# Squares of q's first block and the norm of the latent keys in small pieces on ScalarE, the keys' transposes inside the index loop

## The reference

```
n = rms_norm(h, norm1_g)
q_att, c_kv, q_idx, k_idx, w_idx, r_q, r_k, r_v, r_gate, g_att, g_ret = split(n @ w_in)
q = rms_norm(q_att.reshape(B, S, 8, 128), q_norm_g)
kv = rms_norm(c_kv, kv_norm_g) @ w_kv_up
k_sh, v_sh = split(kv, 2)
k_sh = rms_norm(k_sh, k_norm_g)
k_idx = rms_norm(k_idx, idx_k_norm_g)
dots  = einsum('bqhd,bsd->bqhs', q_idx, k_idx) * IDX_DIM ** -0.5
score = einsum('bqhs,bqh->bqs', relu(dots), w_idx)      # causal, then top_k(score, 256)
logits = einsum('bqhd,bqkd->bhqk', q, k_sel) - slopes * dist
```

## Time and profile before

| | |
|---|---|
| median of 3 runs | 1596.65 us (1596.41 to 1597.43) |
| profiled execution, its own time | 1592.75 us |
| its span, first to last instruction | 1590.9 us |
| TensorE busy | 1464.6 us, 92% |
| VectorE busy | 1093.0 us, 69% |
| ScalarE busy | 768.1 us, 48% |
| POOL busy | 494.7 us, 31% |
| mean granted TensorE clock | 0.964 |

### The profile page before, as it was taken

One profiled execution on the slowest core, in us unless ns is written; L12 is line 12 of the kernel. 1 busy time (PEld: TensorE's weight loads), 2 busy tenths in 40 slices (PEclk: granted clock), 3 DMA queues, 4 the chain that ended last, 5 costly groups with the idle time before them and its releaser, 6 DMA issues.

```text
span 1590.9 us, 19861 instructions
## 1 busy us (share of the span) xinstructions
PE 1464.6 (92%) x7190; PEld 1210.8 (76%) x7190; DVE 1093.0 (69%) x1530; ACT 768.1 (48%) x1247; POOL 494.7 (31%) x365
## 2 busy tenths in 40 slices
PE   5989899998999797999999999999996699999895
PEld 5978788986889686677687888888874677877784
DVE  4328999999999467765378843336354778988783
ACT  5237223337322626766442442333244577878783
POOL 2310121470524135100145543332241234544421
PEclk9999999999999997999999999999998799999998
DMA  5200121112221112210246334434434788798775
GB/s 191 61 27 1 34 49 39 40 41 93 80 53 41 41 40 94 80 41 14 67 150 200 95 132 147 151 139 143 165 116 177 274 296 262 189 297 252 241 229 128
DMA packets 87216, 195.19 MB, mean 123 GB/s; under 512 B 11088, under 2 KB 32848, under 8 KB 84816
## 3 DMA queue, kind: packets, MB, share of 16 engines
q1 hardware_dynamic: 74448, 153.56, 28.8%
q0 software_dynamic: 8928, 32.51, 8.5%
q10 hardware_dynamic: 3744, 7.87, 1.3%
HBM read 200.71 MB, written 37.22 MB: 150 GB/s over the span
## 4 chain that ended last, share of the span: by engine, by line
PE 70%; DVE 10%; DMA 8%; ACT 5%; issue 3%; SPq 1%; POOL 1%; ACTq 0%; DVEq 0%; POOLq 0%
PE ps L718 20%; PE ps L720 19%; PE ps L719 19%; PE ps L940 4%; DMA e_raw<-in_w_up 3%; DVE dist L1576 2%; DMA out<-e_y,dest 2%; PE ps L930 2%; DVE e_lo L1961 2%; PE ps L1049 1%; DMA w_raw<-in_w_in 1%; ACT junk L1227 1%; DMA xin<-in_x 1%; DVE f_sum L1694 1%; PE ps L883 1%
## 5 line engine op out<-in xcount | busy, mean ns | idle before, releaser
L2018 POOL TENSOR_TENSOR w_lo<-w_raw,w_hi 128x512 fp32r<-128x512 f32 (+1 forms) x184 | 257.1, 1403 | 642.4 <-ACT w_hi L1117 641.8
L1117 ACT CAST w_hi<-w_raw 128x512 fp32r<-128x512 f32 (+1 forms) x184 | 111.9, 615 | 419.2 <-PE ps L720 369.2
L718 PE MATMUL ps<-w_hi,n_hi 128*128 128x512 f32 (+2 forms) x704 | 246.2, 350 | 8.6 <-POOL w_lo L2018 6.8
L719 PE MATMUL ps<-w_lo,n_hi 128*128 128x512 f32 (+2 forms) x704 | 243.4, 346 | 0.0
L720 PE MATMUL ps<-w_hi,n_lo 128*128 128x512 f32 (+2 forms) x704 | 243.2, 346 | 0.0
L1961 DVE TENSOR_TENSOR e_lo<-e_raw,e_hi 128x2048 fp32r<-128x2048 f32 x93 | 210.1, 2286 | 28.7 <-ACT e_hi L1468 27.2
L1468 ACT CAST e_hi<-e_raw 128x2048 fp32r<-128x2048 f32 x93 | 176.3, 1916 | 67.0 <-DMA e_raw<-in_w_up 66.8
L1613 DVE MAX8 small<-dist 128x8 f32<-128x384 f32 (+5 forms) x192 | 171.8, 895 | 6.6
L1614 DVE MATCH_REPLACE8 dist<-small,dist 128x384 f32<-128x384 f32 (+5 forms) x192 | 168.1, 876 | 0.0
L718 PE MATMUL ps<-n_hi,w_hi 128*128 128x512 f32 x416 | 164.2, 395 | 3.0 <-POOL w_lo L2018 2.9
L719 PE MATMUL ps<-n_lo,w_hi 128*128 128x512 f32 x416 | 162.3, 390 | 0.0
(11 more groups left out here) (272 smaller groups left out, 2872.1 us busy)
## 6 DMA issues: line engine op xcount, KB each, us to landing
e_raw<-in_w_gate SPq DMA_DIRECT2D x62, 512.0 KB
e_raw<-in_w_up SPq DMA_DIRECT2D x62, 512.0 KB
e_raw<-in_w_down SPq DMA_DIRECT2D x31, 1024.0 KB
w_raw<-in_w_in SPq DMA_DIRECT2D x120, 256.0 KB, 2.7
a_raw<-att_dram SPq DMA_DIRECT2D x16, 512.0 KB, 3.4
a_raw<-ret_dram SPq DMA_DIRECT2D x16, 512.0 KB, 3.4
w_raw<-in_w_out SPq DMA_DIRECT2D x24, 256.0 KB, 3.2
w_raw<-in_w_in SPq DMA_DIRECT2D x40, 128.0 KB, 2.3
```

The source lines that it names most:

```text
L718: mm(out, a[0], b[0], start=first, stop=False, skip_group_check=skip)
L719: mm(out, a[0], b[1], start=False, stop=False, skip_group_check=skip)
L1117: nc.scalar.copy(w_hi[c % NH][:, :width], split_from(c)[:, :width]).then_inc(hi_ready, 1)
L2018: G.tensor_tensor(w_lo[c % NH][:, :width], split_from(c)[:, :width], w_hi[c % NH][:, :width].bitcast(F32), ALU.subtract).then_inc(lo_ready, 1)
```

## The change

Three things are rearranged.

1. The norm of the latent keys. Squares and scaling leave VectorE. ScalarE squares and sums tile h's keys after the relu of step (3, h) (`square_k`), and scales them after the relu of step (4, h) (`norm_k`); `norm_k(0)` waits for POOL, whose two instructions now follow the last square. `k_sq` and `k_n` count to 8.
2. The keys' transposes. TensorE's eight, ScalarE's `kT_hi` and VectorE's `kT_lo` move from behind the index loop to the start of t = 6 (`KT_TILE`). So that they find banks 6 and 7, the strips of t = 2 to 5 begin with bank pair 6, 7 instead of 0, 1.
3. q's squares. `square_q0(t)` now does one tile, after ScalarE's cast at chunk t of gate1.

```diff
+        k_junk = [r1t(f"k_junk{i}", [P, DH], 2624 + i * DH) for i in range(2)]
...
+        KT_TILE = 6
         for t in range(2, NT):
+            if t == KT_TILE:
+                for half in range(2):
+                    bk.use(("kT", half), 6 + half)
             for h in range(HI):
-                bk.use(("idx", t, h), 2 * (h % 4), 2)
-        for half in range(2):
-            bk.use(("kT", half), 6 + half)
+                bk.use(("idx", t, h), 2 * ((h + (3 if t < KT_TILE else 0)) % 4), 2)
...
+            def turn_k():
+                pe.wait_ge(k_n, NT)
+                for half in range(2):
+                    bk.wait_free(pe, ("kT", half))
+                    for t in range(4):
+                        last = tr(bank(("kT", half))[:, t * P:(t + 1) * P], kvu[:, 4 * half + t, 0:DH], ident)
+                    bk.filled(last, ("kT", half))
...
             for t in range(2, NT):
+                if t == KT_TILE:
+                    turn_k()
...
-            pe.wait_ge(k_n, 1)
-            for half in range(2):
-                bk.wait_free(pe, ("kT", half))
-                for t in range(4):
-                    last = tr(bank(("kT", half))[:, t * P:(t + 1) * P], kvu[:, 4 * half + t, 0:DH], ident)
-                bk.filled(last, ("kT", half))
...
+            def square_k(t):
+                if t == 0:
+                    for i in range(4):
+                        bk.wait_read(act, ("kvu", i))
+                if t >= 2:
+                    act.wait_ge(k_sq, t - 1)
+                A(k_junk[t % 2][:], kvu[:, t, 0:DH], ACT.Square, accum_out=small[:, 48 + t:49 + t]).then_inc(k_sq, 1)
+
+            def norm_k(t):
+                if t == 0:
+                    act.wait_ge(k_rstd, 1)
+                A(kvu[:, t, 0:DH], kvu[:, t, 0:DH], ACT.Identity, scale=small[:, 56 + t:57 + t]).then_inc(k_n, 1)
...
             for t in range(2, NT):
+                if t == KT_TILE:
+                    turn_k()
...
                     bk.read(A(relu[n % 2][:, :nk], ps[:, c:c + nk], ACT.Relu), name)
                     n += 1
+                    if t == 3:
+                        square_k(h)
+                    if t == 4:
+                        norm_k(h)
...
             def out_block(name):
-                ahead(name)
+                for k in range(KT):
+                    hi(number[name] * KT + k + NH - 1)
+                    if name == "gate1":
+                        square_q0(k)
...
-                if (what, m) == ("phase2", 1):
-                    square_q0()
...
-            ksq = sq[:].rearrange("p t d -> p (t d)")[:, 0:S].rearrange("p (t d) -> p t d", d=DH)
-            seq(V.tensor_tensor(ksq, kvu[:, :, 0:DH], kvu[:, :, 0:DH], ALU.mult))
-            V.tensor_reduce(small[:, 48:56], ksq, X, ALU.add).then_inc(k_sq, 1)
-            dve.wait_ge(k_rstd, 1)
-            V.tensor_tensor(kvu[:, :, 0:DH], kvu[:, :, 0:DH], small[:, 56:64].unsqueeze(2).to_broadcast([P, NT, DH]), ALU.mult).then_inc(k_n, 1)
...
             for t in range(2, NT):
+                if t == KT_TILE:
+                    lo_kT()
...
-            pool.wait_ge(k_sq, 1)
+            pool.wait_ge(k_sq, NT)
```

More of the change, by code:

```diff
@@ L1167, in _, with turn_k @@
                 bk.read(nc.scalar.copy(kvu[:, 2 * i:2 * i + 2, :].rearrange("p t d -> p (t d)"), bank(name)), name)
+            def square_k(t):
[9 more added lines that the diff above has]
+                A(kvu[:, t, 0:DH], kvu[:, t, 0:DH], ACT.Identity, scale=small[:, 56 + t:57 + t]).then_inc(k_n, 1)
+            def turn_k():
+                for half in range(2):
+                    name = ("kT", half)
+                    bk.wait_full(act, name)
+                    A(kT_hi[:, half * BANK:(half + 1) * BANK], bank(name), ACT.Identity,
+                      scale=gains[:, GK:GK + 1]).then_inc(kT_hi_done, 1)
             n = 0
             for t in range(2, NT):
+                if t == KT_TILE:
+                    turn_k()
                 nk = (t + 1) * P
@@ L1178, in _ @@
                     n += 1
-            for half in range(2):
-                name = ("kT", half)
-                bk.wait_full(act, name)
-                A(kT_hi[:, half * BANK:(half + 1) * BANK], bank(name), ACT.Identity,
-                  scale=gains[:, GK:GK + 1]).then_inc(kT_hi_done, 1)
+                    if t == 3:
+                        square_k(h)
+                    if t == 4:
+                        norm_k(h)
             def out_gate(p):
@@ L1614, in take_rounds @@
                     seq(V.match_replace(sc, m8, sc, TAKEN))
-            for half in range(2):
-                name = ("kT", half)
-                dve.wait_ge(kT_hi_done, half + 1)
-                bk.read(V.scalar_tensor_tensor(kT_lo[:, 4 * half:4 * half + 4], bank(name).rearrange("p (t k) -> p t k", k=P), gains[:, GK:GK + 1],
-                                               kT_hi[:, half * BANK:(half + 1) * BANK].rearrange("p (t k) -> p t k", k=P).bitcast(F32),
-                                               ALU.mult, ALU.subtract), name)
             for t in range(NT):
```

30 lines of the change are left out of this document (17 added, 13 removed).

## The result

The change took 1579.05 us (median of 4 runs, 1577.75 to 1580.16) against 1596.53 us of the kernel before in the same comparison (4 runs, 1595.24 to 1597.43): ratio 0.9898, 95% interval 0.9885 to 0.9911, a gain of 17.5 us. The forecast was 1579.9 with a range of 1576.0 to 1587.0 and faster at 0.95: right, and most of its terms can be found again in the trace. Two of them can't: the squares of k were mis-sized, and VectorE's slack before head 2 came out half as wide as forecast. One sentence of it failed as well: the granted clock in the index loop did not rise. That the time came within 0.9 us of the forecast is partly luck.

What follows compares the result with a forecast made beforehand. TensorE, busy for 92% of the span, was taken as the bound between 110 and 620 us. Gate0 -7.1, gate1 -10.1 and its end +0.4 summed to -16.8 us: 1579.9 us from the median of 1596.65, range 1576 to 1587.

Steps and rivals of the forecast that it cites:

- squares of k, t = 3: Index loop, t = 3: eight squares on ScalarE lengthen the steps, +1.4 us, bounds 0.7 and 2.
- POOL's wait: Index loop before t = 4: ScalarE's first scaling waits for POOL and delays VectorE, +1.9 us, from 1.0 to 3.0.
- gate0's first chunk (A): Behind the index loop: gate0's first chunk ends at 167.6 instead of 174.7, -7.1 us, bounds -5 and -8.5.
- gate1: Block gate1: the cast ahead of q's squares removes 6.97 us of waiting and 3.1 of low clock, -10.1 us.
- end of gate1: Behind gate1's last cast: the last four squares delay the Silu, TensorE may be late, +0.4 us.
- VectorE's wait left at 543: Before head 2: VectorE's 19.4 us wait for POOL shrinks by 15.0, leaving 4.4 us.
- The clock in the loop: Index loop's start: without TensorE's 4.56 us wait the half clock of 119 to 125 us goes, hidden behind VectorE's pace.
- The turn's place: Keys' turn at t = 6: transposes hidden, the 4.0 us wait gone, gate0 follows at once at full clock.
- Rival (c): Index loop: the clock falls and the kernel gets slower, +33 us if t = 3 to 7 ran at 1.2 GHz; chance 0.03.
- (a): Rival, index loop: it gives back what it gains, so gate0 gains nothing, time 1587; chance 0.10.
- (b): Rival, before head 2: VectorE becomes the bound at 543, time 1581 to 1585; chance 0.04.
- (d): Rival, gate1: the stall is only moved, POOL or ScalarE late one chunk later, 1586 to 1590; chance 0.03.

Runs made afterwards that it cites:

- e6: Changed kernel with each square of k in the index loop taken a second time into an unread buffer; 1578.0 us, one run.
- e4: Changed kernel with the keys' turn back behind the index loop and the old bank order; ratio 0.9926 to the kernel before.
- e0: The changed kernel itself, run again without edits; ratio 0.9892 to the kernel before, median 1578.08 us.
- e2: Changed kernel with q's squares back in one block ahead of gate1; ratio 0.9956 to the kernel before.
- e3: Changed kernel with squares, sums and scaling of k back on VectorE ahead of the loop; ratio 0.9918 to the kernel before.
- e5: Changed kernel with the eight scalings of k three steps later; ratio 0.9878 to the kernel before, median 1575.33 us.
- e7: Changed kernel with four more max instructions on VectorE before round 0 of the last tile's top-k; 1581.47 us, one run.
- e10: The kernel of e5 (changed kernel, scalings of k three steps later) run again beside e9; ratio 0.9882 to the kernel before, median 1578.03 us.
- e9: The changed kernel itself a third time, without edits, as partner of e10; ratio 0.9885 to the kernel before, median 1578.45 us.
- e1: Kernel before with part 3 alone, q's squares four at a time behind gate1's casts; ratio 0.9944 to the kernel before.

## Why the prediction was right, point by point

| term (changes in us, measured in the changed kernel's first profile) | predicted | measured |
|---|---|---|
| VectorE's start | -5.1 | -5.25 |
| t = 2 | 0 | +0.42 |
| squares of k, t = 3 | +1.4 | 0 |
| POOL's wait, t = 4 | +1.9 | +1.86 |
| `kT_lo` in the loop | +1.5 | +1.33 |
| last relu, the sum of those above | -0.3 | -1.66 |
| gate0's first chunk (A), loop included | -7.1 | -8.25 |
| gate1 | -10.1 | -9.95 |
| end of gate1 | +0.4 | 0 |
| A, gate1 and its end together | -16.8 | -18.2 |
| VectorE's wait left at 543 | 4.4 | 2.32 |

- **The step that was mis-sized** is "Relu and square together are 1.03 us, 0.17 us over the step". It added the relu's full duration to the squares' spacing in gate1. In that row each square waits for the one before; in the loop neighbours overlap by 0.1 us at both ends. The prediction had the overlap in hand (it used it for the scalings, from four casts in 2.18 us) and didn't apply it to the squares. The eight squares at t = 3 cost 0 us instead of 1.4. That is more than the 1.15 us by which A was better than forecast; the pause at t = 2 took 0.42 back. e6 shows the right price.
- **POOL's wait** was right in sum, for slightly other reasons. POOL's first instruction took 0.70 us instead of the 0.20 of the earlier trace rows, so ScalarE stood still 1.91 us and not 1.35. With the first scaling, 0.31 from its start to the relu's, ScalarE was 2.22 us late, and VectorE passed on 1.86 of them. The prediction's own parts, 1.35 and 0.30, add up to less than its 1.9. Its sentence that ScalarE can't catch up within t = 4 was wrong: behind the stall the relus start 0.88 us apart, against a step of 0.98.
- **The clock in the loop** is the sentence that failed. The prediction had the end of TensorE's wait of 4.56 us remove the half clock of 119 to 125 us. The wait went, and the half clock came all the same, at 121 to 127 us and twice more. It had put its price at nothing, as VectorE sets the pace, and that held up to t = 5.
- **The turn's place**, with gate0 following at once, was right: a TensorE wait of 3.99 us, the transposes at low clock and the low clock behind them went together, and the row of e4 brings them back. The transposes inside the loop hid as forecast, with `kT_lo` ending TensorE's one longer wait there, 1.44 us, after it had made three strips of t = 6. The Trainium skill's rule that transposes don't count as work for the clock gate (TensorE: Matmul & The Clock Gate, Part 4: PE-mode transpose) would have allowed a fall there that costs time. There is a low stretch at 147 to 151 us, behind the transposes, in the changed kernel, and one near it in e0, e2, e3, e5 and e7 to e10; e4, without transposes in the loop, has none there, which agrees with the rule. But e4 lacks the wait for `kT_lo` as well, and the low stretch begins in that wait or right behind it, 4 to 7 us behind the transposes, with strips between them; e6, with both, has none. So it isn't settled which of the two brings it. The price was nil in the changed kernel's first execution and 0.4 us in e0 and 0.3 in e9, under the 1.6 us that the prediction had named for this rule.
- **Rival (c)** was right in its mechanism and wrong in its price. The clock fell inside the loop as the Trainium skill warns (TensorE: Matmul & The Clock Gate, A second HAM failure mode: psum-queue depth-cycling), but TensorE runs up to four bank pairs ahead and VectorE sets the pace, so 0.67 over 10 us and 0.89 over the next 33 cost the changed kernel nothing one can find, and e0 and e9 0.3 to 0.4 us. The prediction's sum for a clock of 1.2 GHz throughout shows why: by it a step of t = 3 takes TensorE 1.28 us (an eighth of 10.2) against VectorE's 0.86, so each step at half clock uses up 0.42 us of TensorE's lead, and only then is VectorE late. Whether short pauses bring the clock down, as that section says of another kernel, no run here shows.
- **The end of gate1** cost nothing, as the eight Silu ran in 4.03 us behind full banks instead of 5.31.
- **Spread in the sum.** The 18.2 us are 1.4 more than forecast, but about 1.5 of them hang on the longer half clock in before's one profile of gate1 (see e2), and in e0 and e9 the shift at B is 17.2 us.
- **The slack at 543** came out 2.1 us smaller than forecast: TensorE gained 1.4 us more than its sum, and VectorE's rounds ended only 1.1 us earlier, not 1.8. VectorE's rows about the loop's end show where its time went, changed kernel:

```profile
166.31 1.27 DVE L1608 TENSOR_TENSOR dist<-dist,cst 128x128 f32<-128x128 f32 x1
167.61 1.20 DVE L1649 TENSOR_SCALAR dist<-cst 128x128 f32<-128x128 f32 x1
168.85 0.29 DVE L1650 TENSOR_TENSOR dist<-dist,cst 128x128 f32<-128x128 f32 x1
```

POOL beside them:

```profile
165.20 3.53 POOL L2040 TENSOR_TENSOR w_lo<-w_raw,w_hi 128x512 fp32r<-128x512 f32 x2 [37.62 <-ACT w_hi L1124]
```

The mask addition takes 0.29 us in every other key tile and 1.27 here, where POOL is splitting weights; POOL's two, one row here, take 2.23 and 1.34 us instead of 1.29. Before, the mask addition ran with POOL idle; the row of 1.20 us behind it is no loss, as before it took 1.25, also beside a split of POOL's. The same happens once more at 385.49, where VectorE's 768 wide `SCALAR_TENSOR_TENSOR` (L1664) takes 1.93 us against 0.96 before, under POOL's instruction at 385.12. The rounds' own `MAX8` and `MATCH_REPLACE8` show nothing of the kind. Work of POOL's that now lies beside these two instructions thus took about 2 us from VectorE; that the two engines exclude each other there is read from these rows and not tried by an experiment.

The other rivals: (a) was out by the trace, the loop gave back 3.6 us of 5.25, and A gained 8.25 all the same. (b) missed by 2.3 us, and e7 shows that its mechanism is real. (d) is out by e1.

## What to carry to other kernels

Work given to an engine between the instructions of a loop costs what its start-to-start spacing adds, not its duration: 0.48 and 0.29 us for a relu and a square that the trace lists as 0.60 and as 0.30 with a 0.19 read, and it is free up to the step of the engine that sets the pace. Where such work needs another engine's answer, put as many steps between question and answer as the answer takes; three steps made a stall of 1.9 us vanish in the traces, though the medians can't tell the two kernels apart. And when TensorE is sped up at two places at once, look for the next engine's slack behind both: here 19.4 us of it shrank to 2.3, and a gain beyond that has to be won for VectorE as well.

## What the runs showed of the hardware

- VectorE and POOL lengthen each other's instructions: 1.27 us for 0.29 and 1.93 for 0.96 on VectorE, 2.23 for 1.29 on POOL. The Trainium skill (SBUF — State Buffer, SBUF: two separate sides) says that the two share a pair of ports as an exclusive lock, held for a whole instruction, also where VectorE reads two operands from SBUF and POOL's instruction reads SBUF. The rows agree: the mask addition ends 0.15 us behind POOL's first split, the row after it 0.08 behind the second, and the 768 wide one goes on for 0.81 us behind POOL's, nearly its own 0.96. POOL's 0.20 us instruction that took 0.70 at t = 4 fits as well: it ends 0.05 us behind a `SCALAR_TENSOR_TENSOR` of VectorE's.
- The granted clock fell to 0.50 in a stretch in which TensorE was busy for 9.8 of 10 us by the profile, with no listed pause above 0.2 us (pauses of a tenth or two wouldn't show). Making its strips a third wider didn't prevent it. In kernels with nearly the same loop, and in executions of the same kernel, the first fall lasted from about 7 us (changed kernel) to about 14 (e0).
- In these traces such a fall cost time only where it left VectorE waiting for TensorE's strips: nothing for 7 to 14 us at half clock where VectorE set the pace, and 0.1 to 0.5 us for a fall of 3 to 7 us that had begun by 0.5 us behind TensorE's restart from a wait.
- The 31 expert tiles, with the same instructions, took, with the token product ahead of them, 355 to 363 us in different executions; a single profiled span hides or invents 4 us for that reason.
